# Norm chains in halves of 512 columns in a four-layer encoder kernel with hi/lo split weights

## The reference

```python
for i in range(DEPTH):                       # DEPTH = 4
    h = rms_norm(x, attn_norm[i])
    x = x + mixer(h, w_in[i]) @ w_o[i]
    x = x + conv_ffn(rms_norm(x, ffn_norm[i]), w_up[i], conv_w[i], conv_b[i], w_down[i])
    gate = sigmoid(rms_norm(x, ple_norm[i]) @ w_ple_gate[i])
    x = x + gate * (p[i] @ w_ple_proj[i])
```

## Time and profile before

| | |
|---|---|
| time of 3 runs | 1390.23 us median (1387.05 to 1390.9) |
| profiled execution | 1385.67 us, span 1383.7 us |
| PE busy | 1327.9 us, 96% of the span |
| DVE, ACT, POOL busy | 69%, 59%, 30% |
| mean granted TensorE clock | 0.989 of full speed |
| DMA | 232.88 MB, mean 168 GB/s |

### The profile page before, as it was taken

One profiled execution on the slowest core, in us unless ns is written; L12 is line 12 of the kernel. 1 busy time (PEld: TensorE's weight loads), 2 busy tenths in 40 slices (PEclk: granted clock), 3 DMA queues, 4 the chain that ended last, 5 costly groups with the idle time before them and its releaser, 6 DMA issues.

```text
span 1383.7 us, 24542 instructions
## 1 busy us (share of the span) xinstructions
PE 1327.9 (96%) x8340; PEld 1174.7 (85%) x8340; DVE 957.6 (69%) x1467; ACT 823.1 (59%) x1421; POOL 413.9 (30%) x499
## 2 busy tenths in 40 slices
PE   6999999999999999999996799999999999999998
PEld 5788999988878799998875689998878788999886
DVE  5777777745777777774588577776376777777535
ACT  5776666643667666663465566665366776666433
POOL 4541233300265123330037213332004521333200
PEclk9999999999999999999997899999999999999999
DMA  8533565564564455565553055556456335556651
GB/s 286 187 118 128 178 183 180 185 196 160 198 213 153 137 183 182 184 182 196 175 165 109 16 168 183 182 182 196 169 175 198 123 122 168 183 182 183 199 166 61
DMA packets 64022, 232.88 MB, mean 168 GB/s; under 512 B 7280, under 2 KB 7408, under 8 KB 63952
## 3 DMA queue, kind: packets, MB, share of 16 engines
q1 hardware_dynamic: 61056, 221.87, 49.6%
q0 software_dynamic: 2896, 10.08, 2.6%
HBM read 230.87 MB, written 1.05 MB: 168 GB/s over the span
## 4 chain that ended last, share of the span: by engine, by line
PE 72%; DVE 14%; ACT 4%; DMA 3%; issue 3%; POOL 3%; SPq 0%; POOLq 0%; ACTq 0%; DVEq 0%
PE bank L1272 20%; PE bank L1248 16%; PE bank L1250 16%; PE bank L1249 16%; DVE w_lo L716 6%; DMA w_raw<-weights 3%; PE bank L1397 2%; DVE tok L763 2%; ACT w_hi L427 1%; DVE hT_lo L771 1%; DVE x L736 1%; PE bank L1420 1%; ACT tok L609 1%; ACT tok L448 1%; POOL rstd L1099 1%
## 5 line engine op out<-in xcount | busy, mean ns | idle before, releaser
L716 DVE TENSOR_TENSOR w_lo<-w_raw,w_hi 128x1024 fp32r<-128x1024 f32 x418 | 550.1, 1353 | 126.9 <-ACT w_hi L427 126.6
L427 ACT ACTIVATE w_hi<-w_raw 128x1024 fp32r<-128x1024 f32 x418 | 421.6, 1054 | 142.8 <-PE bank L1272 110.8
L1248 PE MATMUL bank<-hT_hi,w_hi 128*128 128x256 f32 x1408 | 398.7, 283 | 1.2 <-DVE hT_lo L771 1.2
L1249 PE MATMUL bank<-hT_lo,w_hi 128*128 128x256 f32 x1408 | 398.4, 283 | 0.0
L1250 PE MATMUL bank<-hT_hi,w_lo 128*128 128x256 f32 x1408 | 398.4, 283 | 0.0
L1248 PEld LDWEIGHTS bank<-hT_hi,w_hi 128*128 128x128 f32 x1408 | 270.3, 192 | 2.9 <-issue 2.9
L1250 PEld LDWEIGHTS bank<-hT_hi,w_lo 128*128 128x128 f32 x1408 | 270.3, 192 | 0.0
L1249 PEld LDWEIGHTS bank<-hT_lo,w_hi 128*128 128x128 f32 x1408 | 270.3, 192 | 0.0
L1234 POOL TENSOR_TENSOR gate_c<-gate_c,up_c 128x256 f32<-128x256 f32 x88 | 108.4, 1232 | 285.4 <-ACT gate_c L691 285.4
L1066 DVE SCALAR_TENSOR_TENSOR gate_c<-bank,conv_sb,gate_c 128x255 f32<-128x255 f32 (+1 forms) x176 | 84.1, 478 | 118.6 <-ACT up_c L687 118.6
L1248 PE MATMUL bank<-w_hi,hT_hi 128*128 128x512 f32 (+1 forms) x336 | 134.9, 401 | 7.5 <-DVE hT_lo L771 6.8
(11 more groups left out here) (139 smaller groups left out, 2020.6 us busy)
## 6 DMA issues: line engine op xcount, KB each, us to landing
w_raw<-weights SPq DMA_DIRECT2D x418, 512.0 KB, 4.2
gain<-gains POOLq DMA_DIRECT2D x11, 512.0 KB, 4.9
rel<-rel_in POOLq DMA_DIRECT2D x8, 256.0 KB, 3.4
x<-x_in SPq DMA_DIRECT2D x2, 512.0 KB, 6.1
p_raw<-p_in POOLq DMA_DIRECT2D x4, 256.0 KB, 5.1
out<-x SPq DMA_DIRECT2D x2, 512.0 KB, 2.6
gain<-gains SPq DMA_DIRECT2D x1, 512.0 KB, 6.2
consts<-consts_in POOLq DMA_DIRECT2D x1, 392.0 KB, 5.2
```

The lines of the kernel that those rows point to most:

```text
L427: nc.scalar.activation(w_hi[:, slot, q * HALF:(q + 1) * HALF], w_raw[:, raw, :], ACT.Copy).then_inc(hi_ready, 1)
L716: nc.vector.tensor_tensor(w_lo[:, slot, cols], w_raw[:, half(q)[0], :], w_hi[:, slot, cols].bitcast(F32), ALU.subtract).then_inc(lo_ready, 1)
L1248: nc.tensor.matmul(out_ap, l_hi, r_hi, start=start, stop=False, skip_group_check=True)
L1249: nc.tensor.matmul(out_ap, l_hi, r_lo, start=False, stop=False, skip_group_check=True)
```

## The change

Norm chain in halves: `add_tile` and `add_gated` announce `x_ready` after each 512 columns; the square is two instructions of 512 columns with a sum each, and POOL adds the two sums ahead of its other two operations; the normalise is two instructions, and PE's four transposes of a bank wait for their own half. The last unit of every pass (attention output, down, gate, both tiles) is done bank by bank by `last_rows_unit`, which announces bank 0 as `half_done`; adds and sigmoids wait per bank. In `norm` and ahead of norm 3L+1 half splits are moved between the steps. The output is stored in four DMAs of 256 KB.

```diff
@@ wait_tile
-        def wait_tile(engine, update, t):
-            if t == 0:
+        def wait_tile(engine, update, t, b):
+            if b == 0:
+                engine.wait_ge(half_done, 2 * update + t + 1)
+            elif t == 0:
                 engine.wait_ge(tile_done, update + 1)
             else:
                 engine.wait_ge(unit_used, LAST_UNIT[update] + 1)
@@ sync: output
-                sp.wait_ge(x_ready, 2 * (3 * DEPTH - 1) + t + 1)
-                sp.dma_start(out[t * P:(t + 1) * P, :], x[:, t, :]).then_inc(stored[t], 16)
+                for b in range(2):
+                    c = slice(b * 512, (b + 1) * 512)
+                    sp.wait_ge(x_ready, 4 * (3 * DEPTH - 1) + 2 * t + b + 1)
+                    sp.dma_start(out[t * P:(t + 1) * P, c], x[:, t, c]).then_inc(stored[t], 16)
@@ scalar: square, sigmoids, norm
-                nc.scalar.activation(tok[:, t, :], x[:, t, :], ACT.Square, scale=D ** -0.5,
-                                     accum_out=ssq[:, t:t + 1]).then_inc(ssq_ready, 1)
+                for b in range(2):
+                    c = slice(b * 512, (b + 1) * 512)
+                    if n:
+                        act.wait_ge(x_ready, 4 * (n - 1) + 2 * t + b + 1)
+                    elif b == 0:
+                        act.wait_ge(x_landed[t], 16)
+                    ins = nc.scalar.activation(tok[:, t, c], x[:, t, c], ACT.Square, scale=D ** -0.5,
+                                               accum_out=ssq[:, t, b:b + 1])
+                ins.then_inc(ssq_ready, 1)
...
-                wait_tile(act, 3 * L + 2, t)
                 for b in range(2):
+                    wait_tile(act, 3 * L + 2, t, b)
...
                 if before:
                     before(0)
-                square(n, 0)
-                for u in units[:-2] or units[:1]:
-                    split_next(u)
+                    split_half(units[0], 0)
+                    square(n, 0)
+                    split_half(units[0], 1)
+                    split_next(units[1])
+                else:
+                    square(n, 0)
+                    for u in units[:-2]:
+                        split_next(u)
                 round_hT(n, 0)
@@ vector: add_tile, normalise, norm, ahead of norm 3L+1
-                wait_tile(dve, n - 1, t)
                 for b in range(2):
                     c = slice(b * 512, (b + 1) * 512)
+                    wait_tile(dve, n - 1, t, b)
+                    nc.vector.tensor_tensor(x[:, t, c], x[:, t, c], row_bank(n, t, b)[:, :], ALU.add).then_inc(x_ready, 1)
...
-                nc.vector.scalar_tensor_tensor(tok[:, t, :], x[:, t, :], rstd[:, t:t + 1], gain[:],
-                                               ALU.mult, ALU.mult).then_inc(tok_ready, 1)
+                for b in range(2):
+                    c = slice(b * 512, (b + 1) * 512)
+                    nc.vector.scalar_tensor_tensor(tok[:, t, c], x[:, t, c], rstd[:, t:t + 1], gain[:, c],
+                                                   ALU.mult, ALU.mult).then_inc(tok_ready, 1)
...
                 add(0)
-                normalise(n, 0)
-                for u in units[:-2] or units[:1]:
-                    split_next(u)
-                rest_hT(n, 0)
                 if n % 3 == 0:
+                    split_half(units[0], 0)
+                    normalise(n, 0)
+                    split_half(units[0], 1)
+                    split_half(units[1], 0)
+                    rest_hT(n, 0)
+                    split_half(units[1], 1)
                     add(1)
-                if units[:-2]:
                     split_next(units[-2])
-                if n % 3:
+                else:
+                    normalise(n, 0)
+                    for u in units[:-2]:
+                        split_next(u)
+                    rest_hT(n, 0)
+                    split_next(units[-2])
                     add(1)
...
                 split_next(FIRST_O[L] + 1)
-                split_next(FIRST_O[L] + 2)
+                split_half(FIRST_O[L] + 2, 0)
                 add_tile(n1, 0)
+                split_half(FIRST_O[L] + 2, 1)
                 add_tile(n1, 1)
@@ gpsimd: norm_rstd
+                    own.inc(nc.gpsimd.tensor_tensor(ssq[:, t, 0:1], ssq[:, t, 0:1], ssq[:, t, 1:2], ALU.add))
+                    own.wait()
-                    rsqrt(rstd[:, t:t + 1], ssq[:, t:t + 1], 1, rstd_ready)
+                    rsqrt(rstd[:, t:t + 1], ssq[:, t, 0:1], 1, rstd_ready)
@@ tensor: transpose_tok, the new last_rows_unit
-                pe.wait_ge(tok_ready, 2 * n + t + 1)
                 for b in range(2):
+                    pe.wait_ge(tok_ready, 4 * n + 2 * t + b + 1)
...
+            def last_rows_unit(first, k, count, t, left_hi, left_lo, banks):
+                slot = (first + k) % RING
+                ts = slice(t * P, (t + 1) * P)
+                for b in range(2):
+                    for j in range(2):
+                        c = 2 * k + j
+                        for l, w in ((left_hi, w_hi), (left_hi, w_lo), (left_lo, w_hi)):
+                            col = j * D + b * 512
+                            last = nc.tensor.matmul(banks[2 * t + b][:, :], l[:, c, ts], w[:, slot, col:col + 512], start=False,
+                                                    stop=(j == 1 and l is left_lo), skip_group_check=True)
+                    if b == 0:
+                        last.then_inc(half_done, 1)
+                return last
```

More of the change, by code:

```diff
@@ L750, in add_gated @@
                     own.wait()
[L751 to L754 removed]
+                    nc.vector.tensor_tensor(x[:, t, c], x[:, t, c], tok[:, t, c], ALU.add).then_inc(x_ready, 1)
             def normalise(n, t):
@@ L1285, in second_pass @@
                         transpose_tok(next_norm, 0)
-                    rows_unit(first, k, count, 1, left_hi, left_lo, acc).then_inc(unit_used, 1)
+                    rows = last_rows_unit if k == ks[-1] else rows_unit
+                    rows(first, k, count, 1, left_hi, left_lo, acc).then_inc(unit_used, 1)
             pe.wait_ge(ident_landed, 16)
@@ L1449, in o_piece @@
                     pe.wait_ge(o_ready, PAIRS * L + 2 * k + 2)
-                    last = rows_unit(FIRST_O[L], k, ROW_UNITS, t, hT_hi, hT_lo, o_banks)
+                    rows = last_rows_unit if k == ROW_UNITS - 1 else rows_unit
+                    last = rows(FIRST_O[L], k, ROW_UNITS, t, hT_hi, hT_lo, o_banks)
                     if t == 1:
@@ L1507, in _ @@
                     pe.wait_ge(gT_ready, FC * L + 2 * k + 2)
-                    last = rows_unit(FIRST_DOWN[L], k, DOWN_UNITS, 0, gT_hi, gT_lo, acc)
+                    rows = last_rows_unit if k == tail[-1] else rows_unit
+                    last = rows(FIRST_DOWN[L], k, DOWN_UNITS, 0, gT_hi, gT_lo, acc)
                 last.then_inc(tile_done, 1)
@@ L1515, in _ @@
                         transpose_tok(n0 + 2, 1)
-                    last = rows_unit(FIRST_GATE[L], k, ROW_UNITS, 0, hT_hi, hT_lo, acc)
+                    rows = last_rows_unit if k == ROW_UNITS - 1 else rows_unit
+                    last = rows(FIRST_GATE[L], k, ROW_UNITS, 0, hT_hi, hT_lo, acc)
                 last.then_inc(tile_done, 1)
```

21 lines of the change are left out of this document (5 added, 16 removed).

## The result

The changed kernel takes 1381.67 us (median of 11 runs, 1380.27 to 1387.29). The kernel before, run beside it, takes 1387.45 us (11 runs, 1386.28 to 1394.14). The ratio is 0.9949, 95% interval 0.9935 to 0.9962: faster by 0.5%, 5.8 us. A second comparison on another occasion gave 0.9964 (0.9949 to 0.998), with medians of 1385.65 us after and 1389.63 us before.

The account below looks back on a forecast made before the run. PE, busy 96% of the span, bounds the kernel; about 56 us idle. Terms -3.85 + 0 + 0.3 - 1.8 + 0.4 = -4.95 us, 0.36% off the profiled 1385.67; the same share of median 1390.23 gives 1385.3, range 1382 to 1391.

Parts of the forecast that it names:

- (a): Norm after attention's output projection, four times: wait for `tok` goes, up projection starts sooner; gain 3.85 us, bounds 0 to 5.8.
- (b): Norm before the gate, four times: PE's 0.50 us wait for `w_lo` unchanged; sum 0, bounds gain 0.1, loss 0.4 each.
- (c): Norm of the next layer, three times: 0.90 us `hT_lo` wait goes, given back at `w_lo`; loss 0.3 us in all.
- (d): Program's tail: last add 1.34 us sooner, last output DMA about 0.5 shorter; gain 1.8 us, bounds 1.3 and 2.6.
- The 0.6 that the prediction names beside its 0.5: Last output DMA: saving by the skill's SWDGE (gpsimd) pricing, about 2.0 us fixed and the rest by bytes.
- last add ends 3 us after PE's last matmul: Sign expected in the changed profile at the program's end.
- Start: First norm: tile 1's chain later, delaying weight loads; loss 0.4 us taken, 0.6 if passed through, 0 if bandwidth limits.
- The third rival: Norms behind projections: POOL and DVE exclude each other, so the kernel is slower; over 0.3% from 0.85 us each; chance 0.07.
- Nearly everywhere else PE never stops: Outside the listed waits PE runs on beside weight splits and DMAs, so only norms and the end can pay.
- All waits of (a) gone and the tail at its best: Lower end of the range for the whole kernel: -8 us, 1382 us.
- a microsecond and a half on top: Upper end of the range: added to the slower rival for the spread of runs (1387.05 to 1390.9), giving 1391.

Follow-up runs that it names:

- `tail_only`: Kernel before with only the end changed: layer 3's last gate unit bank by bank, sigmoids per bank, output in four DMAs; 1386.65 us, ratio 0.9986.
- `move_only`: Kernel before with one DVE move ahead of norm 3L+1: tile 0's adds go between two half splits; no halved norm steps or bank order; 1385.69 us, ratio 0.9964.
- `fix_ab`: Changed kernel with rest of `hT` for both tiles ahead of weight halves (norm 3L+1), half the last gate unit split earlier (norm 3L+2); 1381.74 us, ratio 0.9952.
- `old_splits_c`: Changed kernel with the old order of half splits in norm 3L+3; 1381.44 us, ratio 0.9955 to the kernel before.
- `one_sum`: Changed kernel with the square whole again (1024 columns) and no addition on POOL; 1381.07 us, ratio 0.9948 to the kernel before.
- `start_sum_whole`: Changed kernel with a whole square and no POOL addition at the first norm only; 1382.3 us, ratio 0.9953 to the kernel before.
- `before_again`: The kernel before, unedited, profiled a second time; 1387.96 us.

## Why the prediction was right, and where it failed

- **(a)** Forecast: no wait for `tok`, one of about 0.6 for `hT_lo`, adds of tile 0 at 476.4, up projection at 487.4. Measured, less the 1.43 us by which this execution is later: adds 476.49, up projection 487.34, wait 0.49. Gain 4.13 us for the four against this page of before, 3.8 against the mean of 21.01 us over twelve such stages in three executions with the old order (the two of before and `tail_only`); forecast 3.85. What the forecast left unsaid is that the move alone is enough: `move_only` has all of it but 0.05 us a layer.
- **(b)** Forecast: sum 0.4 sooner, POOL 0.3 longer, normalise 0.13 longer, `w_lo` unchanged. Measured: 0.40 (from the last add's end to the sum, 1.18 before and 0.78 after), 0.28 (341.68 to 341.96), 0.13 (next start 1.33 instead of 1.20 us behind), and 4.66 instead of 4.65 us in all. Each term was right. What was read wrongly is the size of the prize: the 0.50 of the earlier trace rows is the idle time of PEld, and taking it away in `fix_ab` gained 0.21 us a layer.
- **(c)** Forecast: 0.90 for `hT_lo` gone and given back whole at `w_lo` two units on, 0.1 later than before. Measured: gone, and given back as 0.17 and 0.56; the unit starts 0.10 sooner (0.11 in the other two), not 0.1 later. The moved splits, from which the forecast expected this, were not needed for it: `old_splits_c`, with the old order, doesn't have the wait either. (b) and (c) together: +0.3 us forecast, -0.32 measured, and it is -1.2 with the old order of splits (`old_splits_c`) and -1.4 with whole sums (`one_sum`).
- **(d)** Forecast 1.34 + 0.5; measured 1.32 + 0.62. The median store of 256 KB takes 2.3 us, in the experiments 2.0 to 2.5. The 0.6 that the prediction names beside its 0.5 is a price for DMAs that POOL issues; these are issued by SP, so the agreement is no test of it. The sign "last add ends 3 us after PE's last matmul" doesn't fit the prediction's own times; it is 2.1.
- **Start.** Forecast +0.4: 0.6 if it passes through, 0 if the loads limit. The load is issued 0.6 us later, as forecast; what of it reaches PE is below what differs between executions.
- **The third rival**, POOL held by DVE: the EPS operation at 366.79 lasts 1.08 us and ends 0.08 after DVE's second half split (367.79), as one ended with the normalise before. The third operation took 0.54 us at 482.48, while DVE was normalising, and 1.26 us once in `start_sum_whole`, which cost 0.3; its mean over 24 is 0.286 us, far from the 0.85 per norm that would have decided. By the Trainium skill ("SBUF — State Buffer", section "SBUF: two separate sides") VectorE with two SBUF inputs, as in a weight split, and GpSimd exclude each other for a whole instruction; the rows at 366.79 and 366.54 agree.
- **What bounds the kernel.** "Nearly everywhere else PE never stops" is not so in layer 2's attention: from 724 to 798 us of before PE is busy for 54.36 of 74 us, at a mean granted clock of 0.82. A third of the 56 idle microseconds lies there, and the change doesn't touch it.

**The step that failed is the lower end of the range**, "All waits of (a) gone and the tail at its best: -8 us, 1382". It went wrong in two ways. First, its base: the share was taken of 1390.23 us, the median of three runs, and the same kernel gave 1387.45 over eleven. Of the 3.6 us between forecast and result 2.8 are this. The upper end got "a microsecond and a half on top" for the spread of the runs, the lower end nothing, though the three runs themselves went down to 1387.05. Second, its terms: the prediction's own best bounds are 5.8 for (a) and 2.6 for the tail, and 0.4 for (b) and 0.6 for (c), which it left out. All four give -9.4 us and 1380.8, and the result lies above that.

The sum itself was 0.8 us too small: -4.95 forecast, -5.78 between the medians. Its terms (a) to (d) came to -5.35 us and measured -6.39 (4.13 + 0.32 + 1.94). The term with the wrong sign is (c), +0.3 forecast and, with (b), -0.32 measured.

How near the number came is in part luck either way. In the second comparison the changed kernel's median was 1385.65 us, within 0.4 of the forecast, and the ratio 0.9964, the one that was forecast. The miss of 0.3 us is small beside the 4 us by which the median of one kernel moved; the stages are what bears the mechanism out.

**How far the accounting closes.** From the four ends of attention on, the layers are 5.77 us shorter in the page of after: 4.13 from stage a, 0.32 from bc, 1.32 from the last add. With the shorter store it is 6.39, and the medians differ by 5.78. The rest of a span, start and attention, is too unsteady to place the 0.6 us between them: 407.3 and 410.0 us in the two executions of before, 414.1 and 414.0 in those of after, 408.1 to 413.3 in the other nine. Whether the change costs something there isn't shown. On average it is 1.1 us more in the eight executions with the changed kernel's code than in the five with that of before.

## What to carry to other kernels

Ask of each part of a chain whether anybody waits for it: here a move of two instructions ahead of a half split gave four of six microseconds, a bank order and a smaller store at the very end the other two. Halving a step pays where its first half can run under something else (0.12 us here) and costs where it can't (0.46 us). A wait that vanishes is no gain until the next dependent unit starts sooner, so measure from one fixed point to another past the following wait. Look whose idle time a bracket is: one of the weight loads that run ahead is not one of the matmuls. And a range in microseconds needs the spread of its base, and every term's bound, at both ends.

## What the hardware did that was not expected

After PE had waited 2.65 us for `w_lo` at the start, its granted clock fell to half, the level of 1.2 GHz. Windows of 1 us of the changed kernel (start and end, length, busy us of PE, PEld, DVE, ACT, POOL, then granted clock, DMA share, GB/s):

```profile
27.00:28.00 1.00, 0.63 (x2) 0.59 (x3) 1.00 (x3) 1.00 (x3) 0.00 (x0) 0.86 0.70 238
28.00:29.00 1.00, 1.00 (x4) 0.72 (x4) 0.84 (x2) 0.06 (x1) 0.05 (x1) 0.50 0.85 201
...
30.00:31.00 1.00, 1.00 (x4) 0.81 (x3) 0.00 (x0) 0.00 (x0) 0.95 (x1) 0.50 0.97 393
31.00:32.00 1.00, 1.00 (x5) 0.78 (x4) 0.00 (x0) 0.00 (x0) 0.90 (x1) 0.93 0.80 324
```

PE is busy throughout and does four matmuls in a microsecond at 0.50, six at full speed (2.4 GHz, 32 to 33 us), so a wait of 2.65 us cost about 1.6 more behind it: eight matmuls that start 0.43 us apart instead of 0.23. In before, after a wait of 0.69 us, the clock stays at 1.00. All five executions with a wait of 2.01 us or more at this place show such a fall (that with 2.01 too: 0.93, 0.50, 0.50, 0.50 and 0.86 from 26 to 31 us), the eight with 1.40 or less none.

The length of the wait doesn't decide alone. In layer 3's attention PE waits 1.51 us up to 1087.70 in the page of after, and the clock is 0.54 from 1089 to 1092 us; in that of before it waits 1.49 us up to 1085.82 at the same matmul, and the clock stays at 1.00. Two executions of one kernel can differ in it: from 782 to 794 us, in layer 2's attention, the clock is 1.00 in the page of before and 0.72 in `before_again`, with PE busy for 9.04 and 9.03 us. Such falls are part of what makes start and attention unsteady; how large a part wasn't measured.
